# Expert weights of an encoder block: rows of 16 KB and transfers of 2 MiB, two ring places at a time

## The chip, the cores and the metric

The kernel runs on one core of a Trainium2 chip. The metric is the device time of one execution in microseconds (us). Names used below: PE is TensorE, ACT is ScalarE, DVE is VectorE, SP is SyncE, whose queue issues nearly all transfers. 1 MiB is 1,048,576 bytes; rates are in GB/s of 10^9 bytes.

## What is computed

One layer of a bidirectional encoder over 512 tokens of width 2048, in float32: adaLN modulation, a mixer of two attention branches, an output projection, then an expert-choice feed-forward part and a final RMSNorm. The change is in the feed-forward part. Each of 16 experts picks its 64 best tokens:

```python
def _expert_choice_ffn(h, w_router, w_e_gate, w_e_up, w_e_down):
    b, s, d = h.shape
    cap = EC_CAPACITY * s // N_EXPERTS                       # 64
    logits = jnp.einsum('bsd,de->bse', h, w_router)
    aff = jax.nn.softmax(logits, axis=-1)
    vals, idx = lax.top_k(jnp.swapaxes(aff, 1, 2), cap)
    xg = jax.vmap(lambda hb, ib: hb[ib])(h, idx)
    a = jnp.einsum('becd,edf->becf', xg, w_e_gate)           # 2048 x 1024 each
    u = jnp.einsum('becd,edf->becf', xg, w_e_up)             # 2048 x 1024
    y = jnp.einsum('becf,efd->becd', jax.nn.silu(a) * u, w_e_down)   # 1024 x 2048
    y = y * vals[..., None]
    ...scatter-add of y into the tokens
```

The weights of one expert are 3 x 8 MiB, those of all experts 384 MiB, each read once.

## The kernel before

The part before the experts (adaLN, input projection, attention, output projection) takes the first 1276 us and is written as dense blocks on PE with float32 weights split in two on ACT and DVE. It is touched in one way only: the order of rows inside a tile. With ROWS = 2, row k of a tile of x1 is every second column of a stretch of 256 (`x1_rows[:, k // ROWS, :, k % ROWS]`, line 1026); adaLN vectors, the router's weights and `xn` (line 1549) follow the same order.

The experts run in 8 pairs (PAIRS). The two experts of a pair share PE's array, each with 64 output rows, so that one product `bank[...][64 * e:64 * e + 64]` belongs to expert e. A pair has three stages: gate, up, down. In each stage the 2048 rows (gate, up) or 1024 rows (down) of a weight matrix come in chunks of 1 MiB, 128 partitions x 8 KB, one chunk per expert: 48 chunks per pair (EC), 8 groups of two in each stage (KG). A chunk lies in one of 12 places of a ring in SBUF (`e_slot`, NSLOT); places 0 to 5, 6 to 10 and 11 lie in three stretches of memory, so 0/1, 2/3, 4/5, 6/7 and 8/9 are neighbours and 10/11 are not. The first pair has four chunks (ONCE) in places of their own.

SP issues the chunks in order, each after a wait on `e_used`, the count of chunks that PE has done with; PE adds 2 after each group:

```python
with sp.Fori(2, PAIRS - 1) as p:
    for cc in range(EC):
        sp.wait_ge(e_used, EC * p + cc - NSLOT + 1)
        load_expert_chunk(p, cc, False)
```

PE's order of work in a pair after the first (`pe_pair`): gate groups, with the four scatters of the previous pair's result (`scatter`, lines 1119 and 1120) one after every second group; up groups, with the transposes of the selection (line 1197) after the second; then a gather of the next pair's tokens (line 1099), the transposes of silu(a) * u (line 1213), another gather; then down groups with two more gathers between them. Before each group PE waits on the semaphores of its two chunks (`chunks_full`). The last pair loads its down weights in another order, in rows of 4 KB and 2 KB (`down_half_chunks`, `down_quarter_chunks`), so that its output columns are done one after another.

Of the kernel before, what the change touches and what calls it, by code (L numbers as in the profile page):

```python
# [71 lines left out]
ROWS = 2  # L72
KG = KD // ROWS
DJ = ROWS // 2
EC, NSLOT = 6 * KG, 24 // ROWS
# [38 lines left out]
def encoder_block(nc, x, c, w_ada, b_ada, g_mix, w_in, g_cq, g_ckv, w_uq, w_ukv, g_qn, g_kn,  # L114
# [20 lines left out]
    w_down_last_v = w_e_down[0].rearrange("e (k p j) n -> k e p j n", p=P, j=2 * ROWS)  # L135
# [3 lines left out]
    with ctx:  # L139
# [68 lines left out]
        e_slot = [at("ring", 8 * i * KB, f"e_slot{i}", [P, ROWS, 2 * W]) for i in range(6)]  # L208
        e_slot += [at("AB", (44 + 8 * i) * KB, f"e_slot{6 + i}", [P, ROWS, 2 * W]) for i in range(5)]
        e_slot += [at("ada", 12 * KB, "e_slot11", [P, ROWS, 2 * W])]  # L210
        e_slot += [at("A", o * KB, f"e_first{i}", [P, ROWS, 2 * W]) for i, o in enumerate((12, 20, 28, 36))]
# [11 lines left out]
        def expert_full(p, c):  # L223

            if not (isinstance(p, int) and p == 0):
                return e_full[expert_slot(p, c)], 16 * USES * p + 16 * ((c + 8) // NSLOT)
            if c in ONCE:
                return once_full[ONCE.index(c)], 16
            return e_full[expert_slot(p, c)], 16 * (in_ring(c) // NSLOT) + 16

# [184 lines left out]
        def _(sp):  # L415
# [185 lines left out]
            def load_expert_chunk(p, c, last_pair):  # L601

                stage_of, g, e = c // (2 * KG), c % (2 * KG) // 2, c % 2
                slot = e_slot[expert_slot(p, c)]
                if stage_of == 2 and last_pair and g < KG // 2:
                    rows = slice(g % 2 * ROWS, (g % 2 + 1) * ROWS)
                    dst, src = slot[:, :, :], w_down_last_v[g // 2, 2 * p + e, :, rows, 0:2 * W]
                elif stage_of == 2 and last_pair:
                    jd, u = 2 + (g - KG // 2) // 2, g % 2
                    dst = slot[:, :, :].rearrange("p j (i n) -> p (j i) n", n=W)  # L610
                    src = w_down_last_v[u, 2 * p + e, :, :, jd * W:(jd + 1) * W]
                else:
                    src = (w_gate_v, w_up_v, w_down_v)[stage_of][g][:, ds(2 * p + e, 1), :]
                    dst = slot[:, :, :].rearrange("p j n -> p (j n)").unsqueeze(1)
                sp.dma_start(dst, src).then_inc(expert_full(p, c)[0], 16)

            for cc in range(NSLOT):
                if cc < 4:
                    sp.wait_ge(lo_ready, N_EXP + 2 * cc + 2)
                elif cc == 4:  # L620
                    sp.wait_ge(chunk_used, N_EXP + NSPLIT)
                elif cc == 11:
                    sp.wait_ge(lsub_ready, 1)
                load_expert_chunk(0, cc, False)
            for cc in ONCE[2:]:
                load_expert_chunk(0, cc, False)
            sp.wait_ge(row_done, 8)
            for cc in ONCE[:2]:
                load_expert_chunk(0, cc, False)
            ring = [c for c in range(EC) if c not in ONCE]  # L630
            for n in range(NSLOT, len(ring)):
                sp.wait_ge(e_used, ring[n - NSLOT] + 1)
                load_expert_chunk(0, ring[n], False)
# [7 lines left out]
            for cc in range(EC):  # L641
                sp.wait_ge(e_used, EC * (PAIRS - 1) + cc - NSLOT + 1)
                load_expert_chunk(PAIRS - 1, cc, True)
            sp.wait_ge(xg_ready, KG + 4 * (PAIRS - 1))
# [10 lines left out]
        def _(pe):  # L655
# [447 lines left out]
            def gather_two(g):  # L1103
# [3 lines left out]
                for i in range(ROWS):  # L1107
                    for t in range(T):
                        last = mm(bank[4 + g % 4][:, i * P:(i + 1) * P], xn[:, t, (ROWS * g + i) * P:(ROWS * g + i + 1) * P],  # L1109
# [13 lines left out]
            def chunks_full(p, c):  # L1123

                for e in range(2):
                    pe.wait_ge(*expert_full(p, c + e))

            def up_chunks(p, c, b0, g):

                chunks_full(p, c)  # L1130
                for j in range(ROWS):
                    k = ROWS * g + j
                    for h in range(2):
                        for e in range(2):
                            last = mm(bank[b0 + h][64 * e:64 * e + 64, :], xgT[:, k, e, :],  # L1135
                                      e_slot[expert_slot(p, c + e)][:, j, h * W:(h + 1) * W], start=k == 0, stop=k == KD - 1)
                last.then_inc(e_used, 2)

            def down_chunks(p, c, g):

                chunks_full(p, c)
                for j in range(DJ):
                    k = DJ * g + j
                    for h in range(4):
                        for e in range(2):
                            last = mm(bank[h][64 * e:64 * e + 64, :], heT[:, k, 64 * e:64 * e + 64],  # L1146
                                      e_slot[expert_slot(p, c + e)][:, 2 * j + h // 2, h % 2 * W:(h % 2 + 1) * W], start=k == 0, stop=k == 7)
                last.then_inc(e_used, 2)

            def down_half_chunks(p, c, m):  # L1150

                chunks_full(p, c)
                for j in range(ROWS):
                    k = ROWS * m + j
                    for h in range(2):
                        for e in range(2):
                            last = mm(bank[h][64 * e:64 * e + 64, :], heT[:, k, 64 * e:64 * e + 64],
                                      e_slot[expert_slot(p, c + e)][:, j, h * W:(h + 1) * W], start=k == 0, stop=k == 7)
                last.then_inc(e_used, 2)

            def down_quarter_chunks(p, c, jd, u):

                chunks_full(p, c)
                for i in range(2 * ROWS):
                    k = 2 * ROWS * u + i
                    for e in range(2):
                        last = mm(bank[jd][64 * e:64 * e + 64, :], heT[:, k, 64 * e:64 * e + 64],
                                  e_slot[expert_slot(p, c + e)][:, i // 2, i % 2 * W:(i % 2 + 1) * W], start=k == 0, stop=k == 7)
                last.then_inc(e_used, 2)

            def pe_pair(p, first, last_pair):

                for g in range(KG):
                    k_end = ROWS * (g + 1)
                    if first:
                        if g == 0:
                            pe.wait_ge(row_ready, 8)
                        pe.wait_ge(xg_ready, g + 1)
                    elif g == 0:
                        pe.wait_ge(y32_ready, 4 * p - 2)  # L1180
                        pe.wait_ge(xg_ready, KG + 4 * p)
                    up_chunks(p, 2 * g, 0, g)
                    if first and g + 2 < KG:
                        gather_two(g + 2)
                    if not first and k_end % 4 == 0:
                        scatter(p - 1, k_end // 4 - 1)
                for g in range(KG):
                    if g == 0 and not first:
                        pe.wait_ge(y32_ready, 4 * p)
                    up_chunks(p, 2 * KG + 2 * g, 2, g)  # L1190
                    if ROWS * (g + 1) == 4:
                        if first:
                            pe.wait_ge(xg_ready, KG)
                        else:
                            pe.wait_ge(scat_added, 16 * p)
                        for t in range(T):
                            last = nc.tensor.transpose(bank[4][:, t * P:(t + 1) * P], sel[:, t, :, :], ident[:, :])
                        last.then_inc(selT_done, 1)
                        for t in range(T):
                            last = mm(bank[5][:, 0:2], sel[:, t, :, :], aff[:, t, ds(2 * p, 2)], start=t == 0, stop=t == T - 1)  # L1200
                        last.then_inc(val_done, 1)
# [6 lines left out]
                for h in range(2):  # L1208
                    pe.wait_ge(he_ready, 2 * p + h + 1)
                    dj = 2 * ROWS if last_pair else DJ  # L1210
# [9 lines left out]
                if not last_pair:  # L1220
                    for g in range(KG):
                        down_chunks(p, 4 * KG + 2 * g, g)
                        if DJ * (g + 1) in (4, 6):
                            u = DJ * (g + 1) // 2
                            pe.wait_ge(xg_ready, KG + 4 * p + u - 1)
                            gather(2 + u, u)
                else:
                    for m in range(KG // 2):
                        down_half_chunks(p, 4 * KG + 2 * m, m)
                    for i in range(4):  # L1230
                        down_quarter_chunks(p, 5 * KG + 2 * i, 2 + i // 2, i % 2)
# [18 lines left out]
        def _(act):  # L1250
# [315 lines left out]
            def first_tokens(g):  # L1566

                act.wait_ge(gather_done, g + 1)
                for i in range(ROWS):
                    k = ROWS * g + i  # L1570
# [4 lines left out]
            def tokens(p, u, b):  # L1575

                act.wait_ge(gather_done, KG + 4 * (p - 1) + u + 1)
# [723 lines left out]
```

## Time and profile before

| | |
|---|---|
| median of 3 runs | 2239.74 us (2238.76 to 2244.37) |
| profiled execution | 2237.74 us |
| its span, first to last instruction | 2235.6 us |
| mean granted TensorE clock | 0.993 |
| PE, PEld, DVE, ACT busy | 95%, 62%, 39%, 25% of the span |
| DMA moved | 635.63 MB, mean 284 GB/s |
| chain that ended last | PE 77%, DMA 14%, DVE 5% |

The profiled execution gives the durations; it is 2.0 us shorter than the median of the runs. PE's busy share counts pipelined matmuls and is not its peak rate. The chain that ended last is followed back from the last instruction: where it shows a DMA, PE was waiting for weights at that time.

### The profile page before, as it was taken

What the parts mean: (1) busy time and instruction counts of PE and PEld (TensorE: products, weight loads), DVE (VectorE), ACT (ScalarE), POOL (GpSimd) and SP (SyncE); (2) the same over time, 40 slices, a digit from 0 to 9 for tenths busy, and PEclk for the clock granted to TensorE, in tenths of its full rate; (3) what the DMA queues carried; (4) which work ended last, traced back from release to release, by engine and by line L of the source; (5) the groups of instructions that cost most, each with busy time, mean ns of one, the idle gap of its engine ahead of it and who ended that gap; (6) DMA issues with size and microseconds to landing.
All of it is one profiled execution on the core that took longest, in us unless ns stands there. A gap on an engine that the chain in (4) does not pass through costs nothing.

```text
span 2235.6 us, 26948 instructions
## 1 busy us (share of the span) xinstructions
PE 2128.5 (95%) x10392; PEld 1390.7 (62%) x10392; DVE 869.1 (39%) x1229; ACT 558.4 (25%) x994; POOL 4.7 (0%) x8
## 2 busy tenths in 40 slices
PE   6999999999999999999999899999999989898986
PEld 4787888888877777888888644343434344444432
DVE  4572668666656665435433400202030302021114
ACT  4254442222246654112222411010100100001002
POOL 0000000000000000000000000000000000000000
PEclk9999999999999999999999999999999999999999
DMA  8967775887760100543422699999999999999998
GB/s 324 341 227 254 263 245 188 319 308 278 280 219 21 29 15 1 189 159 126 160 85 77 262 378 421 414 421 422 422 422 422 422 422 422 422 422 422 422 418 310
DMA packets 170008, 635.63 MB, mean 284 GB/s; under 512 B 23070, under 2 KB 36556, under 8 KB 121676
## 3 DMA queue, kind: packets, MB, share of 16 engines
q1 hardware_dynamic: 165324, 626.19, 72.0%
q10 hardware_dynamic: 4608, 8.39, 1.0%
q8 instruction: 52, 0.85, 0.2%
q14 instruction: 24, 0.20, 0.0%
HBM read 621.94 MB, written 12.58 MB: 284 GB/s over the span
## 4 chain that ended last, share of the span: by engine, by line
PE 77%; DMA 14%; DVE 5%; ACT 2%; issue 1%; SPq 1%; DVEq 0%; ACTq 0%
PE bank L704 23%; PE bank L706 13%; DMA e_slot<-in_w_e_up 12%; PE bank L1135 12%; PE bank L1146 9%; PE bank L1099 5%; PE bank L863 4%; PE bank L754 2%; PE bank L949 2%; DMA sh_tile<-in_w_ada 1%; DMA e_slot<-in_w_e_down 1%; PE bank L1119 1%; PE bank L1109 1%; DVE sh_acc L1712 1%; PE bank L937 1%
## 5 line engine op out<-in xcount | busy, mean ns | idle before, releaser
L1135 PE MATMUL bank<-e_slot,xgT 128*64 128x512 f32 x2040 | 457.9, 596 | 51.5 <-DMA e_slot<-in_w_e_up 39.3
L1135 PEld LDWEIGHTS bank<-e_slot,xgT 128*64 128x64 f32 x2040 | 149.7, 137 | 332.7 <-issue 329.0
L1658 DVE TENSOR_TENSOR w_lo<-stage,w_hi 128x1024 fp32r<-128x1024 f32 (+1 forms) x168 | 202.4, 1205 | 322.6 <-ACT w_hi L1257 322.1
L1257 ACT ACTIVATE w_hi<-stage 128x1024 fp32r<-128x1024 f32 (+1 forms) x168 | 175.2, 1044 | 608.9 <-PE bank L704 340.1
L1146 PE MATMUL bank<-e_slot,heT 128*64 128x512 f32 x872 | 193.5, 594 | 0.0
L704 PE MATMUL bank<-hT_hi,w_hi 128*128 128x512 f32 x512 | 159.0, 392 | 0.0
L704 PE MATMUL bank<-hT_lo,w_hi 128*128 128x512 f32 x512 | 157.8, 389 | 0.0
L704 PE MATMUL bank<-hT_hi,w_lo 128*128 128x512 f32 x512 | 157.7, 389 | 0.0
L1726 DVE SCALAR_TENSOR_TENSOR ada_acc<-ada_tile,siluc,ada_acc 128x1024 f32<-128x1024 f32 x120 | 153.9, 1282 | 6.3 <-DMA ada_tile<-in_w_ada 1.2
L2185 DVE TENSOR_TENSOR x<-x,bank 128x512 f32<-128x512 f32 x128 | 79.6, 682 | 175.3 <-PE bank L1120 173.8
L2175 DVE SCALAR_TENSOR_TENSOR y<-bank,val,gt_row 128x512 f32<-128x512 f32 x32 | 22.0, 744 | 321.1 <-PE bank L1146 296.7
L1580 ACT ACTIVATE xgT<-bank,modcol,a 128x128 f32<-128x128 f32 x112 | 42.1, 455 | 400.0 <-PE bank L1099 400.0
L1146 PEld LDWEIGHTS bank<-e_slot,heT 128*64 128x64 f32 x872 | 61.3, 137 | 116.2 <-issue 113.7
L1099 PEld LDWEIGHTS bank<-sel,xn 128*128 128x128 f32 x896 | 102.2, 192 | 17.0 <-issue 17.0
L704 PEld LDWEIGHTS bank<-hT_hi,w_lo 128*128 128x128 f32 x512 | 96.1, 188 | 20.2
L704 PEld LDWEIGHTS bank<-hT_lo,w_hi 128*128 128x128 f32 x512 | 96.1, 188 | 20.1
L704 PEld LDWEIGHTS bank<-hT_hi,w_hi 128*128 128x128 f32 x512 | 95.1, 188 | 18.9
L1099 PE MATMUL bank<-sel,xn 128*128 128x128 f32 x896 | 106.8, 277 | 0.0
L2219 DVE TENSOR_TENSOR sg<-bank,sg 128x512 f32<-128x512 f32 x16 | 10.3, 686 | 199.8 <-PE bank L1135 199.8
L704 PE MATMUL bank<-oT_hi,w_hi 128*128 128x512 f32 x256 | 81.4, 399 | 0.0
L706 PE MATMUL bank<-w_hi,mT_hi 128*128 128x512 f32 x256 | 80.9, 397 | 0.0
L706 PE MATMUL bank<-w_hi,mT_lo 128*128 128x512 f32 x256 | 79.3, 391 | 0.0
(326 smaller groups left out, 2754.7 us busy)
## 6 DMA issues: line engine op xcount, KB each, us to landing
e_slot<-in_w_e_up SPq DMA_DIRECT2D x128, 1024.0 KB, 21.8
e_slot<-in_w_e_gate SPq DMA_DIRECT2D x127, 1024.0 KB, 19.5
e_slot<-in_w_e_down SPq DMA_DIRECT2D x125, 1024.0 KB, 21.7
ada_tile<-in_w_ada SPq DMA_DIRECT2D x160, 512.0 KB, 5.5
stage<-in_w_in SPq DMA_DIRECT2D x96, 512.0 KB, 6.5
stage<-in_w_out SPq DMA_DIRECT2D x32, 512.0 KB, 3.6
sh_tile<-in_w_ada SPq DMA_DIRECT2D x24, 512.0 KB, 9.0
sig_gates<-sig ACTq DMA_DIRECT2D x32, 256.0 KB, 2.0
```

Of the source, the lines that this page charges most:

```text
L704: last = mm(bank[b][:, :], w[:, s, kk, b * P:(b + 1) * P], a[:, k, :], start=first, stop=end)
L706: last = mm(bank[b][:, :], a[:, k, b * P:(b + 1) * P], w[:, s, kk, :], start=first, stop=end)
L754: last = mm(acc, a[:, 2 * cc + kk, b * P:(b + 1) * P], w[:, s, kk, w0:w1], start=first, stop=end)
L863: last = mm(acc, stationary, moving, start=start and n == 0, stop=stop and n == len(operands) - 1)
L949: mm(bank[4][:, :], v, pT[:, kt % 2, :], start=kt == 0, stop=kt == 3).then_inc(pv_done, 1)
L1099: last = mm(bank[b][:, i * P:(i + 1) * P], xn[:, t, (4 * u + i) * P:(4 * u + i + 1) * P], sel[:, t, :, :], start=t == 0, stop=t == T - 1)
L1135: last = mm(bank[b0 + h][64 * e:64 * e + 64, :], xgT[:, k, e, :], e_slot[expert_slot(p, c + e)][:, j, h * W:(h + 1) * W], start=k == 0, st ...
L1146: last = mm(bank[h][64 * e:64 * e + 64, :], heT[:, k, 64 * e:64 * e + 64], e_slot[expert_slot(p, c + e)][:, 2 * j + h // 2, h % 2 * W:(h % ...
L1257: A(w_hi[:, c % NSPLIT, :, 0:width], stage[:, c % NSTAGE, :, 0:width], ACT.Copy).then_inc(hi_ready, 1)
L1658: V.tensor_tensor(w_lo[:, c % NSPLIT, :, 0:width], stage[:, c % NSTAGE, :, 0:width], w_hi[:, c % NSPLIT, :, 0:width].bitcast(F32), ALU.sub ...
L1726: V.scalar_tensor_tensor(ada_acc[:, :], ada_tile[:, k % NADA, :], siluc[:, k:k + 1], ada_acc[:, :], ALU.mult, ALU.add).then_inc(ada_done, 1)
L2185: V.tensor_tensor(x1[:, t, jd * W:(jd + 1) * W], x1[:, t, jd * W:(jd + 1) * W], bank[4 + t][:, :], ALU.add).then_inc(scat_added, 1)
```

## The change

ROWS goes from 2 to 4. A group of a gate or up stage now has 512 rows of both experts instead of 256, and a down group 256 instead of 128: KG is 4, and a group has 4 MiB. From the second pair on, the part of one expert in a group is one unit of 2 MiB in 128 rows of 16 KB (`load_wide_chunk`). It goes by one transfer into two neighbouring places (`e_wide`); the unit whose turn falls on places 10 and 11 goes by two transfers of 1 MiB with rows of 8 KB. SP waits until both places are free, and PE adds 4 to `e_used` after a group of 4 MiB. Before a group PE waits for both units. The ring still has 12 places.

The first pair keeps chunks of 1 MiB (`load_first_chunk`, each half of a 16 KB row) and groups of two. The last pair has units of 2 MiB in gate and up; its down stage keeps the chunks, rows and groups it has (`load_last_chunk`), with one semaphore wait for the two chunks of a group (`last_full`). Counts on `xg_ready`, `gather_done` and `e_used` are written with STEPS (8) instead of KG. Transposes and the layout of the router's weights and adaLN rows follow ROWS.

```diff
-ROWS = 2
+ROWS = 4
 KG = KD // ROWS
 DJ = ROWS // 2
-EC, NSLOT = 6 * KG, 24 // ROWS
+STEPS = KD // 2
+EC, NSLOT = 6 * STEPS, 12
...
+        e_wide = [at("ring", 16 * i * KB, f"e_wide{i}", [P, 4 * 2 * W]) for i in range(3)]
+        e_wide += [at("AB", (44 + 16 * i) * KB, f"e_wide{3 + i}", [P, 4 * 2 * W]) for i in range(2)]
...
+        def wide_slot(m):
+            return (m + 4) % 6
+
+        def wide_full(p, m):
+
+            n = wide_slot(m)
+            count = 16 * USES * p + 16 * ((m + 4) // 6)
+            return [(e_full[2 * n + i], count) for i in range(2 if n == 5 else 1)]
...
+            def load_wide_chunk(p, m):
+
+                stage_of, g, e = m // (2 * KG), m % (2 * KG) // 2, m % 2
+                src = (w_gate_v, w_up_v, w_down_v)[stage_of][g][:, ds(2 * p + e, 1), :]
+                n = wide_slot(m)
+                if n < 5:
+                    sp.dma_start(e_wide[n][:, :].unsqueeze(1), src).then_inc(e_full[2 * n], 16)
+                else:
+                    for i in range(2):
+                        slot = e_slot[2 * n + i][:, :, :].rearrange("p j n -> p (j n)").unsqueeze(1)
+                        sp.dma_start(slot, src[:, :, i * 4 * W:(i + 1) * 4 * W]).then_inc(e_full[2 * n + i], 16)
...
-            for cc in range(EC):
-                sp.wait_ge(e_used, ring[len(ring) + cc - NSLOT] + 1 if cc < NSLOT else EC + cc - NSLOT + 1)
-                load_expert_chunk(1, cc, False)
+            for m in range(EC // 2):
+                sp.wait_ge(e_used, ring[len(ring) + 2 * m + 1 - NSLOT] + 1 if m < NSLOT // 2 else EC + 2 * m + 2 - NSLOT)
+                load_wide_chunk(1, m)
             with sp.Fori(2, PAIRS - 1) as p:
-                for cc in range(EC):
-                    sp.wait_ge(e_used, EC * p + cc - NSLOT + 1)
-                    load_expert_chunk(p, cc, False)
+                for m in range(EC // 2):
+                    sp.wait_ge(e_used, EC * p + 2 * m + 2 - NSLOT)
+                    load_wide_chunk(p, m)
...
+            def up_wide(p, m, b0, g):
+
+                wide_chunks(p, m)
                 for j in range(ROWS):
                     k = ROWS * g + j
...
+                    last = product(bank[b0:b0 + 2], lambda e: xgT[:, k, e, :],
+                                   lambda h, e: wide_columns(m + e, 2 * j + h), k == 0, k == KD - 1)
+                last.then_inc(e_used, 4)
...
+                        up_wide(p, 2 * g, 0, g)
+                        scatter(p - 1, g)
+                    for g in range(KG):
+                        if g == 0:
+                            pe.wait_ge(y32_ready, 4 * p)
+                        up_wide(p, 2 * KG + 2 * g, 2, g)
+                        if g == 0:
                             pe.wait_ge(scat_added, 16 * p)
-                        for t in range(T):
...
+                            selection(p)
```

## Rows read from the trace of the kernel before

**Rows 1.** The page, span in 40 slices: PE busy tenths, and GB/s moved.

```profile
PE   6999999999999999999999899999999989898986
GB/s 324 341 227 254 263 245 188 319 308 278 280 219 21 29 15 1 189 159 126 160 85 77 262 378 421 414 421 422 422 422 422 422 422 422 422 422 422 422 418 310
```

**Rows 2.** Chain that ended last, in order of time: start us, us, what.

```profile
1551.31 22.19 DMA e_slot<-in_w_e_up
...
1585.50 13.88 PE bank L1146 x64
...
2062.74 13.88 PE bank L1146 x64
```

**Rows 3.** DMA queues, 1600 to 2100 us.

```profile
DMA packets 28969, 210.97 MB, mean 422 GB/s; under 512 B 3218, under 2 KB 3218, under 8 KB 3218
```

**Rows 4.** Windows: length; busy us of PE, PEld, DVE, ACT, POOL; PEclk, DMA share, GB/s.

```profile
1585.50:1704.80 119.30, 110.45 (x566) 50.47 (x568) 18.75 (x34) 11.19 (x25) 0.00 (x0) 1.00 1.01 422
1400.00:1404.00 4.00, 4.00 (x20) 1.61 (x17) 0.00 (x0) 0.00 (x0) 0.00 (x0) 1.00 0.87 322
2171.00:2189.00 18.00, 14.81 (x70) 5.75 (x66) 1.29 (x2) 1.13 (x2) 0.00 (x0) 1.00 1.03 408
2192.00:2209.00 17.00, 15.23 (x68) 6.49 (x66) 8.05 (x13) 5.51 (x13) 0.00 (x0) 1.00 1.05 386
662.00:666.00 4.00, 3.96 (x16) 3.59 (x17) 1.18 (x2) 2.17 (x5) 0.00 (x0) 0.58 0.02 4
```

**Rows 5.** Timeline of PE, a steady pair: last up group, first down group.

```profile
1573.63 3.65 PE L1135 MATMUL bank<-e_slot,xgT 128*64 128x512 f32 x16 [1.32 <-DMA e_slot<-in_w_e_up]
...
1585.43 1.08 PE L1146 MATMUL bank<-e_slot,heT 128*64 128x512 f32 x4
```

**Rows 6.** Timeline of SP, single issues at four places: start us, us.

```profile
1285.27 0.33 SPq L615 DMA_DIRECT2D e_slot<-in_w_e_gate  x1
...
1391.33 0.33 SPq L615 DMA_DIRECT2D e_slot<-in_w_e_gate  x1
...
1400.20 0.33 SPq L615 DMA_DIRECT2D e_slot<-in_w_e_gate  x1
...
1409.27 0.33 SPq L615 DMA_DIRECT2D e_slot<-in_w_e_up  x1
```

**Rows 7.** Their landings, from 1285.27 (two), 1391.33, 1400.20 (two), 1409.27: median us.

```profile
e_slot<-in_w_e_gate SPq DMA_DIRECT2D x2, 1024.0 KB, 5.8
...
e_slot<-in_w_e_gate SPq DMA_DIRECT2D x1, 1024.0 KB, 11.6
...
e_slot<-in_w_e_gate SPq DMA_DIRECT2D x2, 1024.0 KB, 7.9
...
e_slot<-in_w_e_up SPq DMA_DIRECT2D x1, 1024.0 KB, 7.7
```

**Rows 8.** Timeline of PE, pair 1: first and second 4 MiB of the gate stage.

```profile
1396.52 7.09 PE L1135 MATMUL bank<-e_slot,xgT 128*64 128x512 f32 x32 [1.80 <-DVE y L2175]
...
1405.57 7.09 PE L1135 MATMUL bank<-e_slot,xgT 128*64 128x512 f32 x32
```

**Rows 9.** Timeline of PE: transposes with steps of 2, 1 and 4.

```profile
1232.83 0.63 PE L1026 MATMUL bank<-ident,x 128*128 128x128 f32 x4
...
1580.89 1.04 PE L1213 MATMUL bank<-ident,sg 128*128 128x128 f32 x8
...
2174.70 1.25 PE L1213 MATMUL bank<-ident,sg 128*128 128x128 f32 x8 [0.88 <-DVE sg L2219]
```

**Rows 10.** Timeline of PE, last pair: first quarter group of the down stage.

```profile
2196.13 3.65 PE L1167 MATMUL bank<-e_slot,heT 128*64 128x512 f32 x16 [1.77 <-DMA e_slot<-in_w_e_down]
```

**Rows 11.** Timeline of PE around an idle stretch in the attention stage.

```profile
659.10 0.40 PE L863 MATMUL bank<-uv_lo,ckvT_hi 128*128 128x256 f32 x2
662.04 0.50 PE L863 MATMUL bank<-uv_hi,ckvT_hi 128*128 128x256 f32 x2 [2.54 <-DVE qr_lo L1962]
...
663.03 0.63 PE L863 MATMUL bank<-uv_hi,ckvT_hi 128*128 128x256 f32 x2
```

More of the change, by code:

```diff
@@ L1121, in scatter, with product @@
                         .then_inc(scat_done, 1)
-            def chunks_full(p, c):
-                for e in range(2):
-                    pe.wait_ge(*expert_full(p, c + e))
-            def up_chunks(p, c, b0, g):
-                chunks_full(p, c)
+            def product(acc, stationary, weights, first, end):
+                for h in range(len(acc)):
+                    for e in range(2):
+                        last = mm(acc[h][64 * e:64 * e + 64, :], stationary(e), weights(h, e), start=first, stop=end)
+                return last
@@ new lines, in first_full, with up_first @@
+            def first_full(c):
+                for e in range(2):
+                    pe.wait_ge(*expert_full(0, c + e))
+                return [e_slot[expert_slot(0, c + e)] for e in range(2)]
+            def up_first(c, b0, step):
+                slots = first_full(c)
+                for j in range(2):
+                    k = 2 * step + j
+                    last = product(bank[b0:b0 + 2], lambda e: xgT[:, k, e, :],
+                                   lambda h, e: slots[e][:, j, h * W:(h + 1) * W], k == 0, k == KD - 1)
+                last.then_inc(e_used, 2)
@@ new lines, in down_first, with wide_chunks, wide_columns @@
+            def down_first(c, k):
+                slots = first_full(c)
+                last = product(bank[0:4], lambda e: heT[:, k, 64 * e:64 * e + 64],
+                               lambda h, e: slots[e][:, h // 2, h % 2 * W:(h % 2 + 1) * W], k == 0, k == 7)
+                last.then_inc(e_used, 2)
+            def wide_chunks(p, m):
+                for e in range(2):
+                    for full, count in wide_full(p, m + e):
+                        pe.wait_ge(full, count)
+            def wide_columns(m, i):
+                n = wide_slot(m)
+                if n < 5:
+                    return e_wide[n][:, i * W:(i + 1) * W]
+                return e_slot[2 * n + i // 4][:, i % 4 // 2, i % 2 * W:(i % 2 + 1) * W]
@@ L1131, in up_chunks @@
+            def up_wide(p, m, b0, g):
+                wide_chunks(p, m)
                 for j in range(ROWS):
                     k = ROWS * g + j
[L1133 to L1141, printed above, removed]
+                    last = product(bank[b0:b0 + 2], lambda e: xgT[:, k, e, :],
+                                   lambda h, e: wide_columns(m + e, 2 * j + h), k == 0, k == KD - 1)
+                last.then_inc(e_used, 4)
@@ L1142, in down_chunks, with down_wide @@
+            def down_wide(p, m, g):
+                wide_chunks(p, m)
                 for j in range(DJ):
                     k = DJ * g + j
[L1144 to L1147, printed above, removed]
-                last.then_inc(e_used, 2)
@@ L1604, in act_pair @@
                 if first:
-                    for g in range(KG):
+                    for g in range(STEPS):
                         first_tokens(g)
```

187 lines of the change are left out of this document (101 added, 86 removed).

## The prediction

> **What bounds the kernel now.** I read the page's 40 slices first. From slice 24 on the DMA digit is 9 and the rate stands at 422 GB/s while PE is still 9 tenths busy, so busy shares do not settle it [rows 1]. The chain in order of time does: up to 1551 us its pieces are PE's; the first DMA wait on `w_e_up` stands at 1551.31, and from 1585.50 to 2062.74 the down stages of five pairs begin 119.3 us apart, four periods in 477.24 us [rows 2]. A pair is 48 transfers of 1 MiB, 50.33 MB; at 421.9 GB/s (210.97 MB in 500 us) that is 119.3 us, the period itself [rows 3]. PE is busy 110.5 us of a pair [rows 4]. So from about 1400 us the chip's DMA stream sets the end, and two things only can move it: the time per MiB, and time in which the stream has nothing queued. The last such time is at 1400 to 1404 us, 322 GB/s [rows 4]: PE set the pace there and freed slots late.
>
> **The change, part by part.**
>
> *Rows of 16 KB.* Packets over 500 us: 28,969, of which 3,218 are small (16 per transfer) and 25,751 are rows of 8 KB; a row is one packet today [rows 3]. The last pair's down weights come in rows of 4 KB, then 2 KB, and run at 408 and 386 GB/s [rows 4]; the pairs run at 422. Per MiB: 2.716 us (2 KB), 2.570 (4 KB), 2.485 (8 KB). Halving the packets saved 0.146 us, then 0.085 us. Each step removes half as many packets as the one before, so I take the next step as half: 0.043 us, 2.442 us per MiB or 429 GB/s. No row is longer than 8 KB before, so this is an extrapolation. Its ends: 0, if the cost is not one per row (the 4 and 2 KB rows are also pieces with steps between them), and 0.085, if the step as a whole repeats.
>
> What gets the new rows: a unit of 2 MiB goes whole unless it falls on ring places 10 and 11, one in six. From pair 1's unit 6 on: 15 of 18 in pair 1, 100 of 120 in pairs 2 to 6, 13 of 16 in the last pair's gate and up, together 128; I leave the first three to the transition below. 125 units, 250 MiB, x 0.043 = **-10.7 us** (ends 0 and -21).
>
> The Trainium skill (DMA: Bandwidth & Descriptors, "Where 436 GB/s comes from") puts the ceiling of the SBUF ports at 435 GB/s. By that ceiling a MiB can't go under 2.41 us, and this term is at most -19 us; 422 GB/s agrees with it in being below it.
>
> *Coarser release.* The ring holds 12 MiB. PE now gives back 4 MiB at the end of a group of 7.1 us, instead of 2 MiB every 3.5 us. In the steady pairs: let F be the landing of the last up group. Its products end at F+7.1 (two times the 3.65 us groups of now), gathers and transposes take 8.2 us more (1573.63+3.65 to 1585.43) [rows 5], the first down group 7.0 us: F+22.3. SP then refills while one more 4 MiB group is queued, which lands at F+3x9.8 = F+29.4. The refill comes 7.1 us before the stream would end. Elsewhere in the pair PE is less behind. How thin may the queue be? The two MiB issued from 1400.20 on land at 1409.6 at last (1400.4 on average, plus 7.9, plus half of 2.485); two more at 2.485 would land at 1414.6, and the refill issued at 1409.27 landed at 1417.0, 2.4 us behind [rows 6, 7]. A lead of 5.3 us costs nothing. So the steady pairs pay **0**; the cover is 7.1 us of queued weights.
>
> *The transition in pair 1, where PE is the slower.* Now: the thirteenth and fourteenth MiB of pair 1 are issued from 1400.20, halfway through PE's 1396.52 to 1403.61, and have landed by 1409.6 [rows 6 to 8]. After: the issue waits for the whole group, 1403.7. Nothing is queued then; two MiB issued from 1285.27 on into an empty queue had landed 7.2 us later (half the gap of issue 0.2, plus 5.8, plus 1.24) [rows 6, 7]: 1410.9, +1.3 us. The next refill is at 1412.7, when 4 MiB issued together end at about 1415.9: a lead of 3.2 us. The nearest row is the refill of 1400.20 itself: issued 2.7 us before the landing of its predecessor (1391.33+11.6 = 1402.9), its two MiB landed 6.7 us after that one instead of 5.0, a loss of 1.7. Between that and nothing at 5.3 I take 0.9. Leads then grow, because PE frees 4 MiB per 9.05 us (1396.52 to 1405.57) [rows 8], against 9.8 of the stream, and still faster in the up stage. **+2.2 us** (ends +1.3 and +4.7).
>
> *Steps of four in the transposes.* ROWS also orders x1's transposes: 16 sets of four now read every fourth value instead of every second. Eight transposes of `sg` took 1.04 us at step 1 and 1.25 at step 4; four of x1 at step 2 take 0.63 [rows 9]. So the change of step costs up to 0.105 us per set, at least nothing: 0 to +1.7, I take **+1.0 us**, on PE's own path in the output projection. In the middle pairs `sg` goes from step 1 to 2: under 0.2 us a pair, behind the weights stream. xn on ACT reads x1 by fours too; its wait is covered by the choice of experts on DVE.
>
> *Moved counts and waits.* The first pair keeps its 1 MiB units; its source rows of 8 KB now lie 16 KB apart. The last pair waits on one semaphore for two chunks, no instruction more. Its PE starts the down stage some 3.5 us later after the last up landing, but its down groups of 3.65 us need 2 MiB each, 5.1 us of stream, so each leaves 1.5 us free (the first quarter group waited 1.77) [rows 10]; four groups take the 3.5 us back before the last quarters set the end. **0.**
>
> *Sum.* -10.7 + 2.2 + 1.0 = -7.5 us. The profiled execution took 2237.74 us (span 2235.6), so 2230.2; the median of the runs shown is 2.0 us above it: **2232.2 us**.
>
> **The rivals.**
>
> *A, the rate stays 422.* The chip cuts the row, or what slowed the short rows was their steps in HBM. For: no long row in the trace. Against: three sizes with costs that halve. Time: +2.2+1.0, 2242.9. Chance 0.17.
>
> *B, the clock opens the ring's gap: slower.* Today PE waits 1.32 us per group [rows 5] in the late up stage; with 4 MiB groups it will wait 9.8-7.1 = 2.7 us in one piece. After 2.54 us of idling the granted clock was 0.58 over 662 to 666 us and pairs of matmuls of 0.40 us took 0.63, toward 1.2 GHz from 2.4 [rows 4, 11]. That lasted some 3 us and would cost PE 1.5 to 2 us: the lead falls from 7.1 to 5.3, and nothing is lost. If it held for whole groups, 14.2 us each, the first down group would end at F+14.2+8.2+7, the lead would be 0, and each of six pairs would pay about 2.2 us of empty queue (7.2 us for two MiB instead of 5.0) and 1.7 of thin refill, 23 us: 2256. It decides once PE loses more than about 4 us between the last landing and the refill. Chance 0.10.
>
> The Trainium skill (TensorE: Matmul & The Clock Gate, "Loop structure matters more than you think") warns of this shape, a DMA wait before every burst of matmuls, after which they run cold. The trace agrees in kind at 662 us; no run yet shows it for this duty.
>
> *C, the long rows are slower.* Neighbouring partitions read HBM 16 KB apart. Nothing in the trace speaks for it; the same step taken with the other sign gives +10.7+3.2: 2253.6. Chance 0.07.
>
> *D, the full step repeats,* 0.085 per MiB: -21.3+3.2, 2221.6. The semaphore packets of a MiB are halved too, which speaks a little for more than half a step. Chance 0.08.
>
> **How the numbers follow.** The forecast has 0.58, with its own range of 2227 to 2236: 0.035 to 0.055 per MiB (-8.8 to -13.8) and the transition and transposes between +1.3 and +5. A measurement of this kernel tells about 0.3%, 6.7 us. The forecast lies just past that: of its 0.58 I give 0.40 to faster and 0.18 to same. Faster: 0.40 + D 0.08 = 0.48. Same: 0.18 + 0.14 of A = 0.32. Slower: 0.03 of A (with the transition at its dear end and more) + B + C = 0.20. The range is 2225 to 2244: it takes in A and leaves out most of B and C and the far side of D.
>
> **What the profile would show.** Rate: windows inside pairs 2 to 6 at about 428 GB/s (five of six units at 429), pair period 117.6 us; at 422 it is A, below it C. Packets: half as many over 8 KB. Transition: a hole of about 4 us in the DMA stream at 1400 us and a thinner one near 1415. Steady pairs: no window under the pair's own rate; PE waits of 2.7 us with clock 1.00 in the up stage. Clock digits under 0.9 there, with DMA windows that dip at the start of the down stage, would be B. Transposes: four of x1 at 0.7 us. The prediction is wrong if the rate doesn't move, or if the ring of three groups runs dry in every pair.

## The result, and the profile after

The changed kernel takes 2253.15 us (median of 6 runs, 2250.24 to 2255.15) against 2239.37 us (6 runs, 2236.24 to 2244.37): a ratio of 1.0053, 95% interval 1.0043 to 1.0063. It is slower by 0.5%; the forecast was 2232.2 us, faster by 0.3%. Its profiled execution took 2250.24 us, span 2248.1 us, 12.5 us more than before. It is the fastest of the six, 2.9 us under their median, so the trace shows a little less than the typical loss.

The experts' part does nearly what was forecast. The chain that ended last, in order of time (start us, us, what), to be held against [rows 2]:

```profile
1378.11 13.88 PE bank L1164 x64
...
1491.22 13.88 PE bank L1164 x64
...
1572.38 21.13 DMA e_wide<-in_w_e_up
1593.65 7.09 PE bank L1164 x32
...
1609.04 13.88 PE bank L1164 x64
...
2080.26 13.88 PE bank L1164 x64
```

The down stages of pairs 2 to 6 now begin 117.8 us apart (2080.26 - 1609.04 = 471.22 for four), where they were 119.3 apart. The DMA queues from 1600 to 2100 us show why, against [rows 3]:

```profile
DMA packets 17122, 213.69 MB, mean 427 GB/s; under 512 B 1904, under 2 KB 1904, under 8 KB 1904
```

Each row of 16 KB is one packet: 15,218 packets that are not small, where there were 25,751, with five sixths of the bytes in long ones. And the windows of a steady pair and of the transition (length; busy us of PE, PEld, DVE, ACT, POOL; PEclk, DMA share, GB/s), against [rows 4]:

```profile
1491.22:1609.04 117.82, 109.70 (x567) 50.88 (x568) 18.75 (x34) 11.19 (x25) 0.00 (x0) 1.00 1.01 427
1416.00:1420.00 4.00, 4.00 (x21) 1.56 (x18) 1.54 (x3) 0.00 (x0) 0.00 (x0) 1.00 0.80 340
1420.00:1424.00 4.00, 4.00 (x19) 2.05 (x16) 0.84 (x2) 0.00 (x0) 0.00 (x0) 1.00 0.33 74
1424.00:1428.00 4.00, 4.00 (x21) 1.36 (x21) 2.24 (x4) 0.63 (x1) 0.00 (x0) 1.00 0.87 365
```

**Where the time went.** Line up the same events in both chains. The first down stage began at 1359.27 before (the next in that series are 1470.16 and, in [rows 2], 1585.50) and begins at 1378.11 now: **+18.8 us before pair 1's weights have any say**. From there to the down stage of pair 2 it is 230.93 us against 226.23, **+4.7**. Then four periods save **6.0**, and the stretch from 2062.74 (now 2080.26) to the end of the span, 172.86 us before and 167.84 now, saves **5.0**. The sum is 18.8 + 4.7 - 6.0 - 5.0 = 12.5 us.

The 18.8 us are found by walking the timeline of PE backwards. Its first gather of the expert part was at 1277.91 and is at 1296.60; the adaLN columns that line 710 (673 before) writes between the dense blocks of the gate projection stood at 596.31 and now at 616.40; and here the trace changes its face. The timeline of PE, changed kernel:

```profile
419.38 3.67 PE L710 MATMUL bank<-ones,ada_acc 128*128 128x1 f32 x16
422.91 1.20 PE L741 MATMUL bank<-hT_hi,w_hi 128*128 128x512 f32 x2
423.91 1.06 PE L741 MATMUL bank<-hT_lo,w_hi 128*128 128x512 f32 x2
424.76 1.06 PE L741 MATMUL bank<-hT_hi,w_lo 128*128 128x512 f32 x2
...
428.17 0.99 PE L741 MATMUL bank<-hT_hi,w_hi 128*128 128x512 f32 x2
429.00 0.63 PE L741 MATMUL bank<-hT_lo,w_hi 128*128 128x512 f32 x2
```

The same place, kernel before:

```profile
414.61 1.93 PE L673 MATMUL bank<-ones,ada_acc 128*128 128x1 f32 x16
416.40 0.71 PE L704 MATMUL bank<-hT_hi,w_hi 128*128 128x512 f32 x2
416.95 0.62 PE L704 MATMUL bank<-hT_lo,w_hi 128*128 128x512 f32 x2
```

Two things are to be seen. The sixteen tiny matmuls (128 columns of `ada_acc` loaded as weights, one column streamed) take 3.67 us instead of 1.93. And the pairs of 512-column matmuls behind them start 0.85 us apart instead of 0.46, for 6 us: PE runs near 1.2 GHz instead of 2.4 (granted clock 0.50 over 423 to 429 us; it is 1.00 for the first 3 us of the set itself), and is back up at 429.00. The windows of the four blocks that follow such a set, changed kernel (columns as above):

```profile
419.50:469.50 50.00, 50.00 (x211) 41.81 (x209) 29.38 (x25) 10.66 (x12) 0.00 (x0) 0.93 0.75 273
469.50:518.30 48.80, 48.80 (x211) 40.87 (x209) 29.46 (x25) 10.66 (x12) 0.00 (x0) 0.97 0.77 279
518.30:566.80 48.50, 48.50 (x211) 40.69 (x209) 29.37 (x25) 10.65 (x12) 0.00 (x0) 0.96 0.78 281
566.80:618.70 51.90, 51.90 (x230) 43.78 (x229) 29.54 (x26) 12.14 (x14) 0.00 (x0) 0.93 0.75 272
```

and the 210 us that hold them, kernel before:

```profile
410.00:620.00 210.00, 210.00 (x975) 175.45 (x974) 136.45 (x119) 52.39 (x61) 0.00 (x0) 1.00 0.81 291
```

From the first of these sets to the one after the fourth block (read in order) was 181.70 us (414.61 to 596.31) and is 197.02 (419.38 to 616.40): **+15.3 us**, of which 4 x 1.74 = 7.0 are the sets themselves and 8.3 the clock. The other 3.5 of the 18.8 are not one mechanism: the first set itself stands 4.8 us later, though nothing before it reads by rows, and 1.4 us come back by the first gather. In the profiles of all kernels here the first set stands between 414.61 and 419.38, in no order of what they change. It goes with the granted clock over the first 165 us: 0.98 in the kernel before, 0.97 in three kernels whose set stands at 415.5 to 416.2, 0.96 in three at 416.2 to 418.0, 0.95 in the changed kernel and in one other (b_cols4), at 419.4 and 419.3. What sets that clock is not shown.

Why this line: the vector of 1024 adaLN values per block lies in `ada_acc` in the order of the weights' columns, and the columns for the gate blocks 2 to 5 are picked with `ada_rows[:, i // ROWS, :, i % ROWS]` (`by_rows`). With ROWS = 4 each of the 128 values that are loaded lies 16 bytes from the next, where it was 8.

### The profile page after: what moved, and what is told of

Its sections match the earlier page's. It is cut to its first block, busy times and chain, and to the rows that moved or that the text cites. A ratio compares the mean times of both kernels' runs of the same rounds, so it can differ in the third digit from the quotient of the medians.

```text
span 2248.1 us, 26491 instructions
## 1 busy us (share of the span) xinstructions
PE 2149.1 (96%) x10394; PEld 1410.5 (63%) x10394; DVE 869.2 (39%) x1229; ACT 565.8 (25%) x994; POOL 4.7 (0%) x8
## 4 chain that ended last, share of the span: by engine, by line
PE 84%; DMA 8%; DVE 5%; ACT 2%; issue 1%; SPq 0%; DVEq 0%; ACTq 0%
PE bank L1164 25%; PE bank L741 23%; PE bank L743 13%; DMA e_wide<-in_w_e_up 6%; PE bank L1136 5%; PE bank L900 4%; PE bank L791 3%; PE bank L986 2%; PE bank L1156 2%; PE bank L1157 1%; PE bank L710 1%; DMA e_slot<-in_w_e_down 1%; PE bank L1146 1%; PE bank L974 1%; DMA sh_tile<-in_w_ada 1%
## 5 line engine op out<-in xcount | busy, mean ns | idle before, releaser
L1164 PE MATMUL bank<-e_wide,xgT 128*64 128x512 f32 x1456 | 401.3, 599 | 47.4 <-DMA e_wide<-in_w_e_up 18.4
L1164 PEld LDWEIGHTS bank<-e_wide,xgT 128*64 128x64 f32 x1456 | 128.5, 137 | 292.5 <-issue 290.1
L1164 PE MATMUL bank<-e_slot,xgT 128*64 128x512 f32 x584 | 210.4, 605 | 0.0
L1164 PE MATMUL bank<-e_wide,heT 128*64 128x512 f32 x672 | 168.7, 595 | 0.0
L1812 DVE SCALAR_TENSOR_TENSOR ada_acc<-ada_tile,siluc,ada_acc 128x1024 f32<-128x1024 f32 x120 | 153.9, 1282 | 6.6 <-DMA ada_tile<-in_w_ada 1.4
L1164 PEld LDWEIGHTS bank<-e_wide,heT 128*64 128x64 f32 x672 | 52.9, 137 | 101.6 <-issue 99.4
L1164 PE MATMUL bank<-e_slot,heT 128*64 128x512 f32 x328 | 95.6, 595 | 2.5 <-DMA e_slot<-in_w_e_down 1.8
L1164 PEld LDWEIGHTS bank<-e_slot,xgT 128*64 128x64 f32 x584 | 63.1, 139 | 32.9 <-issue 32.0
```

Of the source, the lines that this page charges most:

```text
L1164: last = mm(acc[h][64 * e:64 * e + 64, :], stationary(e), weights(h, e), start=first, stop=end)
L1812: V.scalar_tensor_tensor(ada_acc[:, :], ada_tile[:, k % NADA, :], siluc[:, k:k + 1], ada_acc[:, :], ALU.mult, ALU.add).then_inc(ada_done, 1)
```

## The experiments

Theory **S** (for step): the adaLN columns, read with a step of four, cost 13 us or more, half as longer loads and half as lost clock; the long rows themselves give what was forecast. Its rivals: the early part is later for other reasons (chance, or the changed layout of memory), or the experts' part loses more than its rows save.

**The step alone, in the kernel before (b_cols4).** Only the adaLN columns are read with a step of four; the expert weights keep their 1 MiB chunks.

```diff
-                ada_rows = ada_acc[:, :].rearrange("q (k p j) -> q k p j", p=P, j=ROWS)
+                ada_rows = ada_acc[:, :].rearrange("q (k p j) -> q k p j", p=P, j=4)
...
-                    piece = ada_rows[:, i // ROWS, :, i % ROWS] if by_rows else ada_acc[:, i * P:(i + 1) * P]
+                    piece = ada_rows[:, i // 4, :, i % 4] if by_rows else ada_acc[:, i * P:(i + 1) * P]
```

> The kernel before, with one thing of the change: the weight side of the adaLN column products of four gate blocks reads every fourth value instead of every second (the columns then come in the wrong order; nothing else changes). Theory S (the stride is the loss): each of the four sets of 16 takes 3.67 us instead of 1.9, and the granted clock falls behind each, so that each costs 3 to 5 us in all: 13 to 17 us slower than before, and mean clock about 0.985. Rival W (the loss of the first 1200 us comes from elsewhere in the change, the stretches of low clock being chance): 0 to 7 us slower, clock 0.99.

Measured: 2260.1 us against 2242.19, ratio 1.0078 (1.0057 to 1.0099), 17.9 us slower. The timeline of PE is that of the changed kernel, place for place:

```profile
419.34 3.67 PE L673 MATMUL bank<-ones,ada_acc 128*128 128x1 f32 x16
422.86 1.20 PE L704 MATMUL bank<-hT_hi,w_hi 128*128 128x512 f32 x2
```

Its four blocks take 196.98 us (419.34 to 616.32), +15.3 again. One line that the expert weights don't touch costs more than the whole change does: S stands, and the rivals for the early part fall. The 17.9 us are just above the 13 to 17 that were expected. Part of the excess may lie behind the four blocks: from their end to the first gather it is 684.4 to 685.4 us in three of the four profiles that have slow sets (b_cols4, b_cols8, a_rows8), but 680.2 in the changed kernel, and 680.2 to 683.0 in the five that have no slow set in one piece. The cause of that is open.

**The load's length apart from the clock (a_mixed).** The changed kernel, with the eight columns spread as 3, 3 and 2 between the quarters of the next block's first chunk, so that big matmuls stand between them.

```diff
+                def between(b):
...
+                    for i in ((0, 1, 2), (3, 4, 5), (6, 7), ())[b]:
+                        last = mm(bank[7][:, i:i + 1], rows[:, i // ROWS, :, i % ROWS], ones[:, 0:1], start=True, stop=True)
```

> The changed kernel; the four sets of column products are no longer one piece between two blocks, but three, three and two columns ahead of the first three quarters of the next block's first chunk. Same instructions, same results. Theory S1 (half of the loss is the loads at step 4, 1.8 us a set, the other half the clock, which falls because PE does little else for 3.5 us in one piece): clock 1.00 over the gate blocks, 6 to 9 us faster than the changed kernel, so 5 to 8 us slower than before. Rival S2 (the clock falls whatever stands between the columns): as the changed kernel, 13 to 14 us slower than before.

Measured: 2239.62 us against 2242.19, ratio 0.9996 (0.9984 to 1.0007): some 13 us below the changed kernel (1.0053 less 0.9996, of 2240). Timeline of PE:

```profile
415.88 1.33 PE L728 MATMUL bank<-ones,ada_acc 128*128 128x1 f32 x6
417.07 0.70 PE L757 MATMUL bank<-hT_hi,w_hi 128*128 128x512 f32 x2
...
418.55 1.33 PE L728 MATMUL bank<-ones,ada_acc 128*128 128x1 f32 x6
...
421.22 0.86 PE L728 MATMUL bank<-ones,ada_acc 128*128 128x1 f32 x4
```

The pieces are as slow as before (3.52 us in all), but the pairs behind them take 0.70 and 0.63 us and the granted clock is 1.00 over 410 to 620 us. The four blocks take 188.0 us: 9.0 us of clock are back, 6.3 us of loads remain. So the two halves of S are separate costs, and the second comes from the slow loads standing in one piece. The expectation had the mechanism and missed the size: it said 5 to 8 us slower than the kernel before, and the median shows no difference. By the medians 4 us more are back than the four blocks show. Some 2.9 of them are the choice of run: the changed kernel's profiled execution was that much under its median, a_mixed's was at its median (2239.54).

**The columns contiguous (a_fix).** The changed kernel; DVE's last accumulation of the four rows writes its result in the order of the rows (`ada_by_rows`), so that PE reads 128 neighbouring values. DVE does two instructions on 512 strided values for one on 1024.

```diff
-                    piece = ada_rows[:, i // ROWS, :, i % ROWS] if by_rows else ada_acc[:, i * P:(i + 1) * P]
+                    piece = ada_acc[:, i * P:(i + 1) * P]
...
+                    if by_rows and k == KD - 1:
+                        for g in range(2):
+                            cols = slice(g * W, (g + 1) * W)
+                            out = ada_by_rows[:, cols].rearrange("q (j p) -> q j p", j=ROWS)
+                            tile, acc = (v.rearrange("q (p j) -> q j p", j=ROWS) for v in (ada_tile[:, k % NADA, cols], ada_acc[:, cols]))
+                            last = V.scalar_tensor_tensor(out, tile, siluc[:, k:k + 1], acc, ALU.mult, ALU.add)
```

> The changed kernel, with the last accumulation of each of those four adaLN rows on DVE written in the order in which PE wants it (two instructions that read at step 4 in place of one), so that PE's column products read neighbouring values. Same results. Theory S: the sets take 1.9 us again, clock 1.00 over the gate blocks, about 15 us faster than the changed kernel: 2 us faster to 2 us slower than before. Rival W: no more than 7 us faster than the changed kernel, so 6 us or more slower than before.

Measured: 2232.46 us against 2242.19, ratio 0.9963 (0.9948 to 0.9977). This beats the changed kernel by 0.9% and the one before by 0.4%. It is more than was expected (within 2 us of the kernel before); that expectation took 15 us off the changed kernel, the ratios say 20, of which the four blocks show 15.6. Timeline of PE, and the strided work as DVE's groups from 410 to 620 us (busy us, mean ns, idle before):

```profile
415.53 1.84 PE L712 MATMUL bank<-ones,ada_by_rows 128*128 128x1 f32 x16
417.23 0.72 PE L743 MATMUL bank<-hT_hi,w_hi 128*128 128x512 f32 x2
```

```profile
L1822 DVE SCALAR_TENSOR_TENSOR ada_acc<-ada_tile,siluc,ada_acc 128x1024 f32<-128x1024 f32 x64 | 82.0, 1282 | 2.3
...
L1819 DVE SCALAR_TENSOR_TENSOR ada_by_rows<-ada_tile,siluc,ada_acc 128x512 f32<-128x512 f32 x7 | 7.6, 1124 | 0.1
```

DVE pays for the step instead (1124 ns for 512 values, 1282 for 1024), two such instructions in each of four blocks, 2 x 1.12 - 1.28 = 1.0 us a block. PE does not wait for it: four blocks take 181.47 us. The down stages of pairs 2 to 6 stand 117.8 us apart as in the changed kernel (1591.10 to 2062.30), so nothing of the expert part was touched, and its span, 2230.2 us, is that of a kernel with the new weights' transfers and none of the step's cost.

**The rows alone (a_rows8).** The changed kernel, each 2 MiB unit as two transfers of 1 MiB with rows of 8 KB, under the same waits and groups.

```diff
+                    for i in range(2):
+                        half = slice(i * 4 * W, (i + 1) * 4 * W)
+                        sp.dma_start(e_wide[n][:, half].unsqueeze(1), src[:, :, half]).then_inc(e_full[2 * n + i], 16)
```

> The changed kernel with each unit of 2 MiB sent as two transfers of 1 MiB in rows of 8 KB; places, waits of SP and groups of 4 MiB as changed. Theory R (the rate comes from the rows and transfers): 422 GB/s again, the pair period back from 117.8 to 119.3 us, the end some 9 us later than the changed kernel. Rival (the period fell because of the groups or the waits, not the transfers): 117.8 us.

Measured, one execution: 2262.24 us, span 2260.1, 12.0 more than the changed kernel. Its chain:

```profile
1613.84 13.88 PE bank L1166 x64
...
1733.18 13.88 PE bank L1166 x64
...
1852.47 13.88 PE bank L1166 x64
```

The period is 119.3 us again; the end is 12.0 us later, where 9 were expected. The last period is 122.3 us (to 2094.04), and the trace shows why: behind a wait the last up group takes 10.08 us instead of 7.09, at a lower granted clock, while the DMA rate does not dip.

```profile
2075.66 10.08 PE L1166 MATMUL bank<-e_wide,xgT 128*64 128x512 f32 x32 [2.85 <-DMA e_wide<-in_w_e_up]
```

```profile
2072.00:2084.00 12.00, 9.15 (x30) 2.88 (x28) 0.00 (x0) 0.00 (x0) 0.00 (x0) 0.72 1.01 421
```

 In the other periods the order of the source in HBM (neighbouring partitions 16 KB apart), the ring and the groups are as in the changed kernel; what goes back is the length of the row and the size of the transfer. So the 1.5 us a pair come from these two. They were not tried apart; that 1 MiB transfers with rows of 4 KB and 2 KB are slower yet [rows 4] speaks for the row.

**Pair 1 in narrow groups (a_fix_p1).** a_fix, with chunks of 1 MiB and groups of 2 MiB in pair 1, as before the change: the coarse release begins only with pair 2.

```diff
-            for m in range(EC // 2):
-                sp.wait_ge(e_used, ring[len(ring) + 2 * m + 1 - NSLOT] + 1 if m < NSLOT // 2 else EC + 2 * m + 2 - NSLOT)
-                load_wide_chunk(1, m)
+            for cc in range(EC):
+                sp.wait_ge(e_used, ring[len(ring) + cc - NSLOT] + 1 if cc < NSLOT else EC + cc - NSLOT + 1)
+                load_second_chunk(cc)
...
+            pe_pair(1, False, False)
+            with pe.Fori(2, PAIRS - 1) as p:
```

> The kernel with the rearranged adaLN rows, and in addition the second pair as in the kernel before: units of 1 MiB in rows of 8 KB, groups of 2 MiB, freed two by two; units of 2 MiB from the third pair on. Same results. Theory T (the stream loses its time where PE sets the pace, because a whole group of 4 MiB must be used before the first place comes free): the hole of 322 to 107 GB/s near 1400 us shrinks to that of the kernel before, the down stages of pairs 2 to 6 begin 2 to 3 us earlier than in the run with the rearranged rows alone (40 long-row MiB fewer at 0.037 us cost 1.5 of the 3.5 to 5 us saved), and the end is 2 us earlier: 12 us faster than before. Rival (the hole only moves to where the long units begin): end as with the rearranged rows alone, within 1 us.

Measured: 2231.54 us against 2239.87, ratio 0.9964 (0.9952 to 0.9977), not to be told from a_fix. The windows of the transition, a_fix first, then a_fix_p1:

```profile
1400.00:1404.00 4.00, 4.00 (x22) 1.42 (x18) 0.00 (x0) 0.00 (x0) 0.00 (x0) 1.00 0.25 107
1404.00:1408.00 4.00, 4.00 (x18) 2.05 (x18) 2.94 (x5) 0.63 (x1) 0.00 (x0) 1.00 0.72 221
```

```profile
1400.00:1404.00 4.00, 4.00 (x22) 1.29 (x18) 0.55 (x1) 0.00 (x0) 0.00 (x0) 1.00 0.95 358
1404.00:1408.00 4.00, 4.00 (x18) 1.91 (x16) 2.12 (x4) 0.63 (x1) 0.00 (x0) 1.00 1.01 416
```

The hole is gone, and it has not moved to where the long units begin: from 1408 to 1600 us no window of 4 us is under 401 GB/s. From pair 0's down stage (1361.12; in a_fix 1360.01) to pair 6's it is 700.35 us against 702.29: 1.9 us won by closing it, after what pair 1's short rows give up again. The 2 us that theory T expected at the end are 0.9 by the spans (2229.3 against 2230.2) and nothing by the ratios: it is right on the hole, and its gain at the end is not shown.

**A longer step, and a shorter one (b_cols8, a_cols2).** The same line once in the kernel before with a step of eight, and once in the changed kernel with a step of two as it was.

```diff
-                ada_rows = ada_acc[:, :].rearrange("q (k p j) -> q k p j", p=P, j=ROWS)
+                ada_rows = ada_acc[:, :].rearrange("q (k p j) -> q k p j", p=P, j=8)
```

> The kernel before with the same weight side of the adaLN column products read at step 8 (columns in the wrong order; nothing else changes). If the cost of a step is set by how many values lie in 16 bytes (step 2: two, step 4: one), a set of 16 takes 3.7 us as at step 4. If it grows with the distance, a set takes 5 us or more.

> The changed kernel with the weight side of the adaLN column products read at step 2, as before (columns in the wrong order for the changed layout; all else as changed). Theory S: sets of 1.9 us, clock 1.00 over the gate blocks, 15 us or a little more faster than the changed kernel, and the same end as the run with rearranged adaLN rows, 8 to 10 us faster than before. Rival: if DVE's rearranging in that run took or gave time of its own, the two differ by more than 2 us.

Measured: the step of eight takes 2260.16 us (one execution), 20.3 above the median of the kernel before; the step of two in the changed kernel 2234.81 us against 2239.87, ratio 0.9976 (0.9966 to 0.9985). The first set of each, b_cols8 and then a_cols2:

```profile
417.73 3.74 PE L673 MATMUL bank<-ones,ada_acc 128*128 128x1 f32 x16
```

```profile
416.17 1.93 PE L710 MATMUL bank<-ones,ada_acc 128*128 128x1 f32 x16
```

The set takes 1.84 us contiguous, 1.93 at a step of two, 3.67 at four, 3.74 at eight. It is a level that is reached between 8 and 16 bytes from value to value, not a cost that grows with the distance. a_cols2 has blocks of 181.70 us, to the hundredth those of the kernel before, and is 17 us under the changed kernel by the ratios (1.0053 less 0.9976): the step of four on this one line is the whole of the loss. Against the kernel before it gains 5 us, where 8 to 10 were expected, and it ends 2.9 us behind a_fix by the ratios. The intervals (0.9966 to 0.9985, 0.9948 to 0.9977) overlap, so whether DVE's rearranging gives time of its own is not settled.

## Why the prediction was wrong

**The step that failed is "Steps of four in the transposes".** It followed ROWS to x1's transposes and to `sg` and priced them at +1.0 us (0 to 1.7). The adaLN vectors follow the same order of rows, as the description of the kernel says, but the sum left out what reads them: the products of line 673, four sets of sixteen matmuls on PE's own path. They cost +15.3 us in the trace, and 17 to 20 us by the measured ratios (b_cols4, a_cols2, a_fix). The rule of the step, "up to 0.105 us per set of four", would not have found the size either: scaled to sixteen it gives 0.4 us a set, measured were 1.7, and 2 us of clock behind each.

What was priced there cost nothing. The groups of x1's transposes and of their weight loads, before and after (ns min/median/max, first and last start):

```profile
L1026 PEld LDWEIGHTS bank<-ident,x x64: 195/208/264, 1114.4 to 1257.5; 128*128 128x128 f32 x64
L1026 PE MATMUL bank<-ident,x x64: 270/283/386, 1114.6 to 1257.6; 128*128 128x128 f32 x64
```

```profile
L1063 PEld LDWEIGHTS bank<-ident,x x64: 196/210/261, 1133.2 to 1276.2; 128*128 128x128 f32 x64
L1063 PE MATMUL bank<-ident,x x64: 270/284/386, 1133.4 to 1276.3; 128*128 128x128 f32 x64
```

It would be easy to say that a transpose hides a slow load behind the 128 columns that it streams, while the adaLN products stream one column and leave it bare. The trace does not bear this out: the loads of the transposes are recorded at 208 ns and at 210, so there is no longer load to hide, while those of the adaLN products go from 192 ns in the kernel before to this in a_mixed, at a granted clock of 1.00:

```profile
L728 PEld LDWEIGHTS bank<-ones,ada_acc x64: 308/329/332, 415.7 to 562.6; 128*128 128x128 f32 x64
```

Why the same step slows the one and not the other is open. The two differ in the columns streamed (128 against one), in the kind of instruction and in the tile that is read, and no run here changes one of these alone.

The row for `sg` in [rows 9] (eight at step four, 1.25 us, beside 1.04 at step one) did not carry over. It is the last pair's, behind a wait of 0.88 us, and the changed kernel has 1.26 us there; in its middle pairs, now at step two, the eight take 1.12 us. The trace did hold a better neighbour, the 1.93 us of line 673 beside the 1.84 of the same line read in order: this line answers to the step, and it stands on PE's path four times. The prediction did not look there. But these 0.09 us at a step of two would not have told of the 1.8 us at a step of four.

**Rows of 16 KB, -10.7 us: right, a little large.** 48 MiB in 117.8 us with 8 MiB at 2.485 leave 40 MiB at (117.8 - 8 x 2.485) / 40 = 2.448 us, 0.037 us saved per MiB where the forecast had 0.043. For 250 MiB that is 9.3 us. The halving of the step at each doubling of the row was a fair guess, and no more than a guess. The Trainium skill (DMA: Bandwidth & Descriptors, "Where 436 GB/s comes from") has the ceiling of the ports at 435 GB/s; the 427 GB/s of a pair stay under it, so this trace agrees.

**The transition, +2.2 us: right in its place, larger.** The thirteenth to sixteenth MiB were issued after the whole group, as forecast, and the stream ran nearly dry: 74 GB/s over 4 us. SP's issues there are at 1422.48 (the 2 MiB landed 7.7 us later, forecast 7.2) and 1422.86. Of the 4.7 us that the down stage of pair 2 lost, 3.5 are the longer last up group (its products end 7.1 us after the landing, not 3.65), and the last pair gives those back, as forecast. The rest, 1.2 us, is net of what the long rows already saved in these pairs: 230.93 us would be near 226.23 + 3.5 - 2.4 = 227.3 without a hole, so the hole cost about **3.6 us**, inside the ends of 1.3 and 4.7. The 2.4 is an estimate, 1.6 pairs' share of 1.5.

**Steady pairs and last pair, 0: right.** The slices of the DMA rate from 1600 to 2100 us lie between 419 and 435 GB/s with no dip. The waits of PE (us in total, times, longest):

```profile
PE bank L1164 <- DMA e_wide<-in_w_e_up: 18.4, 13, 2.7
PE bank L1164 <- DMA e_slot<-in_w_e_up: 16.7, 6, 2.8
```

The last two waits of an up stage are 2.7 to 2.8 us in one piece, as forecast; the thirteen of the first row are a mixture, 1.4 us on average. **Rival B came true in the small form that the prediction gave it, and cost nothing.** In the up stages of pairs 3, 5 and 7 the granted clock fell behind the first of these waits. Pair 3, timeline and windows:

```profile
1701.70 0.68 PE L1164 MATMUL bank<-e_wide,xgT 128*64 128x512 f32 x1 [2.78 <-DMA e_slot<-in_w_e_up]
...
1711.49 1.08 PE L1164 MATMUL bank<-e_wide,xgT 128*64 128x512 f32 x4 [1.00 <-DMA e_wide<-in_w_e_up]
```

```profile
1609.04:1726.87 117.83, 111.39 (x566) 51.35 (x568) 18.75 (x34) 11.19 (x25) 0.00 (x0) 0.99 1.01 427
1700.00:1708.00 8.00, 6.29 (x22) 2.45 (x24) 0.00 (x0) 0.00 (x0) 0.00 (x0) 0.79 1.02 433
```

PE is busy 1.7 us longer in such a pair (111.39 against the 109.70 of the pair shown above, whose clock is 1.00). The next wait is shorter by as much, 1.00 us where pair 2 has 2.70, the rate stays at 427 GB/s and the period at 117.8 us. The prediction priced this at 1.5 to 2 us of PE with nothing lost. What it gave 0.10 to, a low clock for whole groups and an empty queue in every pair, did not come. In a_rows8 and a_cols2 the low stretch fell on the last up group, and the down stage began up to 3.0 us later; there too the rate of the stream did not dip. In the kernel before, whose waits for `w_e_up` are at most 1.3 us, no window of 4 us from 1300 to 2224 us is under 0.97. The warning of the Trainium skill (TensorE: Matmul & The Clock Gate, "Loop structure matters more than you think") came true in part: this trace has the low clock behind such a wait, in every second pair and for part of one group, not for every burst.

A and C fall with the rate of 427, D with 0.037. That C's time, 2253.6 us, is nearly the measured 2253.15 is chance: the long rows were not slower.

**The sum without the failed step**, -9.3 + 3.6 = -5.7 us on a span of 2235.6, is 2229.9; a_fix has 2230.2. Its median is 2232.46, where 2232.2 was forecast; that these two nearly meet is partly luck, since the forecast's sum was -7.5 where the runs give -5.7. By ratio to the kernel before it is 0.9963 against 0.9966. What the prediction said of the weights it said rightly in the main, and the kernel was slower because of a line 450 lines above them, tied to them by one constant.

## What to carry to other kernels

When a constant that orders data is changed for the sake of one stage, list every line that reads it, and price each on the engine where it stands; the far ones are not dearer or cheaper for being far. In this kernel a step of four doubled the time of products that load 128 columns and stream one, and left transposes with the same step as they were: price a step from a row of the same kind of instruction, or measure it. And where such slow products stood in one piece they cost twice, since the clock was lower behind them: let the producer (here DVE, hidden) write the order that PE reads, or at least scatter the products among large ones.

## What the runs showed of the hardware

- Sixteen float32 matmuls with 128 loaded columns and one streamed: 1.84 us contiguous, 1.93 at 8 bytes from value to value, 3.67 at 16 bytes, 3.74 at 32. One value per 16 bytes is what costs, and more distance costs nearly nothing. Transposes of x1 at 16 bytes took no longer than at 8 (284 and 283 ns).
- Behind 3.5 to 3.7 us of such matmuls in one piece the granted clock fell and pairs of 512-column matmuls took 1.06 us for 6 us; behind 1.33 us of them, three times with 1.5 us of large ones between, it stayed at 1.00. PE was busy throughout, so a busy PE is not one that keeps its clock.
- Behind waits of 2.77 to 2.78 us for weights, each followed by a group of matmuls, the clock fell in every second pair (0.79 over 8 us) and cost PE 1.7 us. It cost the kernel nothing there: the period stayed at 117.8 us, set by the weights' stream.
- ACT reads at a step of four slowly too. Its `xn` of 2048 values, before and after (ns min/median/max):

```profile
L1549 ACT ACTIVATE xn<-x,rstd x4: 2122/2160/2194, 1262.4 to 1268.5; 128x2048 f32<-128x2048 f32 x4
```

```profile
L1635 ACT ACTIVATE xn<-x,rstd x4: 3932/3948/4010, 1280.9 to 1292.5; 128x2048 f32<-128x2048 f32 x4
```

The last of the four ends at 1296.5 and PE's first gather starts at 1296.60, so the 7.2 us more were just hidden. In a_fix_p1 they were not quite, and PE waited 1.64 us for `xn`. The prediction had said that this wait is covered, without a price for it.
